# Router logits from the raw residual sum, with the norm folded into the router's weights, in a two-layer decoder on one core

## The reference

```python
x = layer_norm(DEEPNORM_ALPHA * x + mix, ln_g[i, 0], ln_b[i, 0])
ffn = grouped_moe(x, router_w, router_b, moe_w_gate[i], moe_w_up[i], moe_w_down[i])

def layer_norm(x, g, b):
    mu = jnp.mean(xf, axis=-1, keepdims=True)
    var = jnp.mean(jnp.square(xf - mu), axis=-1, keepdims=True)
    y = (xf - mu) * lax.rsqrt(var + LN_EPS)
    return y * g + b

# in grouped_moe
probs = jax.nn.softmax(h @ router_w + router_b, axis=-1)    # 32 experts
```

## Time and profile before

| | us |
|---|---|
| median of 3 runs | 1263.96 (1263.32 to 1266.03) |
| the profiled execution | 1266.65 |
| its span, first to last instruction | 1264.8 |
| TensorE busy | 1040.6 (82% of the span) |
| DVE busy | 289.6 (23%) |
| ACT busy | 173.6 (14%) |
| DMA moved | 450.95 MB, mean 357 GB/s |

### The profile page before, as it was taken

The page is one execution under the profiler, slowest core; times in us unless marked ns, Lnnn a source line. Parts: engine busy times, 40 slices in busy tenths (PEclk is TensorE's granted clock), DMA queues, the critical chain, the costliest instruction groups (busy, mean ns, idle before and its releaser), DMA issues.

```text
span 1264.8 us, 18155 instructions
## 1 busy us (share of the span) xinstructions
PE 1040.6 (82%) x7606; PEld 574.9 (45%) x7606; DVE 289.6 (23%) x848; ACT 173.6 (14%) x444; POOL 40.7 (3%) x106
## 2 busy tenths in 40 slices
PE   8999999876669886668899899999866698956675
PEld 6675544543334342233588654535523243523332
DVE  0026331211120211111322685312111111211113
ACT  0014210100000010000121452311100000000001
POOL 2001010000000000000000120100000000000000
PEclk9999999987889997898999899999978899988778
DMA  9943669999999999999985205699999999999994
GB/s 332 399 162 134 265 263 394 412 427 428 427 428 427 427 427 427 427 429 423 379 308 230 104 1 215 268 416 390 427 428 427 427 427 427 427 428 427 427 426 195
DMA packets 53298, 450.95 MB, mean 357 GB/s; under 512 B 4107, under 2 KB 10476, under 8 KB 26076
## 3 DMA queue, kind: packets, MB, share of 16 engines
q1 hardware_dynamic: 50864, 442.51, 84.8%
q0 software_dynamic: 2016, 6.81, 1.5%
q10 hardware_dynamic: 332, 0.40, 0.1%
HBM read 448.63 MB, written 1.07 MB: 356 GB/s over the span
## 4 chain that ended last, share of the span: by engine, by line
PE 47%; DMA 46%; DVE 3%; ACT 2%; issue 1%; SPq 1%; DVEq 0%
DMA ring<-in_moe_w_down 20%; DMA ring<-in_moe_w_up 15%; PE bank L825 12%; DMA ring<-in_moe_w_gate 11%; PE bank L628 7%; PE bank L703 5%; PE bank L876 3%; PE bank L794 3%; PE bank L865 3%; PE bank L635 2%; PE bank L1008 1%; PE bank L675 1%; PE bank L1075 1%; PE bank L1067 1%; PE bank L891 1%; PE bank L691 1%
## 5 line engine op out<-in xcount | busy, mean ns | idle before, releaser
L825 PE MATMUL bank<-ring,work 128*32 128x256 f32 (+1 forms) x2624 | 324.6, 468 | 75.3 <-DMA ring<-in_moe_w_up 35.0
L825 PEld LDWEIGHTS bank<-ring,work 128*32 128x32 f32 (+1 forms) x2624 | 150.9, 128 | 198.6 <-issue 168.5
L876 PE MATMUL bank<-ring,work 128*32 128x512 f32 x576 | 120.5, 784 | 39.0 <-DMA ring<-in_moe_w_down 23.4
L1360 DVE TENSOR_TENSOR xs<-xs,bank 128x512 f32<-128x512 f32 x120 | 76.5, 683 | 293.2 <-PE bank L894 216.0
L1352 DVE TENSOR_TENSOR work<-work,bank 128x256 f32<-128x256 f32 (+1 forms) x32 | 15.6, 488 | 392.3 <-PE bank L825 392.3
L825 PE MATMUL bank<-softmax_area,work 128*32 128x256 f32 (+1 forms) x416 | 67.6, 452 | 29.3 <-DMA ring<-in_moe_w_up 21.2
L628 PE MATMUL bank<-xT,ring 128*128 128x256 f32 x384 | 85.0, 381 | 0.0
L628 PEld LDWEIGHTS bank<-xT,ring 128*128 128x128 f32 x384 | 72.3, 190 | 11.0 <-issue 1.4
L794 PE MATMUL bank<-work,acc 128*128 128x128 f32 (+1 forms) x448 | 73.3, 321 | 4.3 <-DVE xs L1360 4.0
L794 PEld LDWEIGHTS bank<-work,acc 128*128 128x128 f32 x448 | 65.7, 191 | 16.6 <-issue 10.7
L876 PEld LDWEIGHTS bank<-ring,work 128*32 128x32 f32 x576 | 30.9, 137 | 85.7 <-issue 83.2
(11 more groups left out here) (217 smaller groups left out, 1023.1 us busy)
## 6 DMA issues: line engine op xcount, KB each, us to landing
ring<-in_moe_w_gate SPq DMA_DIRECT2D x48, 2048.0 KB, 28.5
ring<-in_moe_w_up SPq DMA_DIRECT2D x42, 2048.0 KB, 28.9
ring<-in_moe_w_down SPq DMA_DIRECT2D x36, 2048.0 KB, 29.8
ring<-in_moe_w_down SPq DMA_DIRECT2D x20, 1024.0 KB, 11.1
bias<-in_moe_w_down SPq DMA_DIRECT2D x8, 2048.0 KB, 32.4
softmax_area<-in_moe_w_down SPq DMA_DIRECT2D x8, 2048.0 KB, 21.1
bias<-in_moe_w_gate SPq DMA_DIRECT2D x8, 2048.0 KB, 31.7
softmax_area<-in_moe_w_up SPq DMA_DIRECT2D x8, 2048.0 KB, 28.4
```

The lines of the kernel that those rows point to most:

```text
L825: last = mm(bank[2 + k][row:row + cap, 0:width], xgT[:, t, at + e * cap:at + (e + 1) * cap], w[e](t)[:, part * width:(part + 1) * width], ...
L876: last = mm(bank[5][row:row + CAP_NARROW, :], hidT_narrow[:, m, CAP_NARROW * e:CAP_NARROW * (e + 1)], w[e](m)[:, n * 512:(n + 1) * 512], s ...
L1360: v.tensor_tensor(c, c, bank[b][:, :], ALU.add).then_inc(acc_added[l], 1)
```

## The change

The normed value of a token is (a - mean) r g + b, with a the raw sum and r the reciprocal deviation. Its product with the router's column is r times the product of a with a centred column, plus a constant. The centred column is g times the router's, less its own sum over features divided by 1024. The constant is the sum of b times the router's column. So the logits can be made from `acc`: the centred weights take the place of `router`, the constant goes into `logit_bias`, and r is multiplied in when DVE takes the logits from PSUM.

- `fold_router` on DVE: two multiplications and two reductions over the eight rows that a partition holds. `sum_router` on TensorE: one product with ones, which adds over partitions. `centre_router` on DVE: two operations. For layer 0 they stand before attention. For layer 1 they stand in pair 4 of layer 0's experts, and GpSimd loads `router_w` again before that.
- Two more small loads bring g and b of the two attention norms by feature (`norm_cols`).
- `norm_tile` leaves `acc` as it is and writes both passes to `xs`.
- TensorE transposes `acc` of tile 0 between the halves of tile 1's output products, and `acc` of tile 1 between the halves of tile 0's logits.
- On ACT the copy of tile 1 into `xT` stands before its square root, and the copy of tile 1 into `xsP` stands after the exponent.
- The wait for small loads is now for all nine.

```diff
...
@@ -547,6 +553,8 @@
             nc.gpsimd.memset(gate_w[:, KT * 3 * HEADS:], 0.0).then_inc(pads_ready, 1)
             pool.dma_start(router[:, 0:KT * E].rearrange("p (t n) -> p t n", t=KT),
                            router_w.rearrange("(p t) n -> p t n", t=KT)).then_inc(small_loaded, 16)
+            for w, src in enumerate((ln_g, ln_b)):
+                pool.dma_start(norm_cols[:, w, :, :], bass.AP(tensor=src.tensor, offset=0, ap=[[KT, P], [2 * D, LAYERS], [1, KT]])).then_inc(small_loaded, 16)
             pool.dma_start(router_bias[:, :], bass.AP(tensor=router_b.tensor, offset=0, ap=[[0, P], [1, E]])).then_inc(small_loaded, 16)
             for b, src in enumerate((nsa_pos_k, nsa_pos_v)):
                 pool.dma_start(pos_rows[:, b, :], src[0].rearrange("(l o) d -> l (o d)", o=2)).then_inc(small_loaded, 16)
@@ -591,6 +599,8 @@
                 load_norm(2 * l + 1)
                 order_columns(l)
                 if l + 1 < LAYERS:
+                    pool.wait_ge(logits_ready, l + 1)
+                    pool.dma_start(router_t, router_w.rearrange("(p t) n -> p t n", t=KT)).then_inc(small_loaded, 16)
                     load_norm(2 * l + 2)
 
 
@@ -602,12 +612,12 @@
                 u = ring_use["fixed", l, n, 0]
                 pe.wait_ge(loaded[slot_no(u)], loads_through(u))
 
-            def transpose_x(n, tt):
+            def transpose_x(n, tt, of=xs):
 
                 after(pe, xT_copied, 2 * (NT * n + tt))
                 for half in range(2):
                     for t in range(4):
-                        last = tr(bank[4 + half][:, t * P:(t + 1) * P], xs[:, tt, 4 * half + t::KT], ident)
+                        last = tr(bank[4 + half][:, t * P:(t + 1) * P], of[:, tt, 4 * half + t::KT], ident)
                     last.then_inc(xT_ready, 1)
 
             def xT_here(n, tt):
@@ -724,28 +734,40 @@
                     for n in range(2):
                         last = out_product(l, m, 1, n)
                 last.then_inc(mix_ready[l], 1)
+                pe.wait_ge(mix_added[l], 2)
+                transpose_x(2 * l + 1, 0, acc)
                 for n in range(2):
                     for m in range(KT // 2, KT):
                         last = out_product(l, m, 1, n)
                     last.then_inc(mix_ready[l], 1)
 
+            def sum_router(l, b):
+
+                pe.wait_ge(router_sums, l + 1)
+                mm(bank[b][:, 0:2 * E], table("ones"), router_red, start=True, stop=True).then_inc(router_psum, 1)
+
             def keep_warm(n, width=512):
 
                 for _ in range(n):
                     mm(bank[2][:, 0:width], ident, tab[:, 0:width], start=True, stop=True)
 
             def route_tokens(l):
-                for tt in range(NT):
-                    normed(l, 0, tt)
-                    transpose_x(2 * l + 1, tt)
-                    if tt == 0:
-                        pe.wait_ge(small_loaded, SMALL_LOADS)
-                        pe.wait_ge(pads_ready, 3)
-                    xT_here(2 * l + 1, tt)
-                    for t in range(KT):
+                def logits(tt, a, b):
+                    for t in range(a, b):
                         last = mm(bank[6][:, tt * P:(tt + 1) * P], xT[:, t, tt * P:(tt + 1) * P], router[:, t * E:t * E + P],
                                   start=(t == 0), stop=(t == KT - 1))
-                last.then_inc(logits_ready[l], 1)
+                    return last
+
+                pe.wait_ge(router_ready, l + 1)
+                pe.wait_ge(small_loaded, SMALL_LOADS)
+                pe.wait_ge(pads_ready, 3)
+                xT_here(2 * l + 1, 0)
+                logits(0, 0, KT // 2)
+                pe.wait_ge(mix_added[l], 4)
+                transpose_x(2 * l + 1, 1, acc)
+                logits(0, KT // 2, KT)
+                xT_here(2 * l + 1, 1)
+                logits(1, 0, KT).then_inc(logits_ready, 1)
                 keep_warm(5)
 
                 pe.wait_ge(chosen_ready[l], 1)
@@ -915,6 +937,9 @@
                     if more:
                         for part in range(2):
                             gather(l, group_of[i] + 1, part)
+                    if i == ROUTER_PAIR and l + 1 < LAYERS:
+                        sum_router(l + 1, 2)
+                        pe.wait_ge(router_ready, l + 2)
                 spread(l, PAIRS - 1)
                 if l + 1 < LAYERS:
                     keep_warm(4)
@@ -1021,6 +1046,8 @@
             first_groups()
             for g in range(2, 6):
                 moba_group(g)
+            sum_router(0, 7)
+
             def moba_job(h, br):
                 if h == 0:
                     pe.wait_ge(proj_dve[0], 3)
@@ -1247,13 +1274,33 @@
                 link(v.bn_aggr(moments[:, tt, :], stats[:, tt, :]))
                 v.tensor_scalar(rstd[:, tt:tt + 1], moments[:, tt, 1:2], EPS, None, ALU.add).then_inc(var_ready, 1)
 
+            def fold_router(l):
+
+                def cols_of(w):
+                    return norm_cols[:, w, l, :].unsqueeze(2).to_broadcast([P, KT, E])
+
+                def over_t(x):
+                    return x.rearrange("p t n -> p n t")
+
+                dve.wait_ge(small_loaded, SMALL_LOADS + 16 * l)
+                link(v.tensor_tensor(router_tmp, router_t, cols_of(1), ALU.mult))
+                link(v.tensor_reduce(router_red[:, E:2 * E], over_t(router_tmp), AX, ALU.add))
+                link(v.tensor_tensor(router_t, router_t, cols_of(0), ALU.mult))
+                v.tensor_reduce(router_red[:, 0:E], over_t(router_t), AX, ALU.add).then_inc(router_sums, 1)
+
+            def centre_router(l, b):
+                dve.wait_ge(router_psum, l + 1)
+                v.tensor_tensor(logit_bias[:, :], router_bias[:, :], bank[b][:, E:2 * E], ALU.add)
+                v.scalar_tensor_tensor(router_t, bank[b][:, 0:E].unsqueeze(1).to_broadcast([P, KT, E]), -1.0 / D, router_t,
+                                       ALU.mult, ALU.add).then_inc(router_ready, 1)
+
             def norm_tile(l, n, tt):
                 k = norm_tiles(l, n, tt)
                 dve.wait_ge(norm_loaded, 32 * (2 * l + n + 1))
-                v.scalar_tensor_tensor(acc[:, tt, :], acc[:, tt, :], moments[:, tt, 0:1], norm_w[:, 0, :], ALU.subtract, ALU.mult)
+                v.scalar_tensor_tensor(xs[:, tt, :], acc[:, tt, :], moments[:, tt, 0:1], norm_w[:, 0, :], ALU.subtract, ALU.mult)
                 dve.wait_ge(std_ready, k)
                 link(v.reciprocal(rstd[:, tt:tt + 1], rstd[:, tt:tt + 1]))
-                v.scalar_tensor_tensor(xs[:, tt, :], acc[:, tt, :], rstd[:, tt:tt + 1], norm_w[:, 1, :], ALU.mult, ALU.add).then_inc(normed_tiles, 1)
+                v.scalar_tensor_tensor(xs[:, tt, :], xs[:, tt, :], rstd[:, tt:tt + 1], norm_w[:, 1, :], ALU.mult, ALU.add).then_inc(normed_tiles, 1)
 
             def attention_norm(l):
                 for tt in range(NT):
@@ -1270,12 +1317,14 @@
                     return x.unsqueeze(2).to_broadcast([P, NT, E])
 
                 pr = route[:, 0, :, :]
-                dve.wait_ge(logits_ready[l], 1)
-                link(v.tensor_tensor(pr, bank[6][:, 0:NT * P].rearrange("p (t e) -> p t e", e=P)[:, :, 0:E],
-                                     router_bias[:, :].unsqueeze(1).to_broadcast([P, NT, E]), ALU.add))
+                dve.wait_ge(logits_ready, l + 1)
+                for tt in range(NT):
+                    last = v.scalar_tensor_tensor(pr[:, tt, :], bank[6][:, tt * P:tt * P + E], rstd[:, tt:tt + 1], logit_bias[:, :],
+                                                  ALU.mult, ALU.add)
+                link(last)
                 link(v.tensor_reduce(one[:, 0, :], pr, AX, ALU.max))
-                v.tensor_tensor(pr, pr, wide(one[:, 0, :]), ALU.subtract).then_inc(logits_shifted[l], 1)
-                dve.wait_ge(logits_exp[l], 1)
+                v.tensor_tensor(pr, pr, wide(one[:, 0, :]), ALU.subtract).then_inc(logits_shifted, 1)
+                dve.wait_ge(logits_exp, l + 1)
                 g4 = pr.rearrange("p t (g e) -> p t g e", e=EG)
                 for a in range(2):
                     v.tensor_tensor(pair_sum[:, :, :, a], g4[:, :, :, 2 * a], g4[:, :, :, 2 * a + 1], ALU.add)
@@ -1399,6 +1448,8 @@
                     more = last_of_group(i) and i + 1 < PAIRS
                     if i == FLAG_PAIR:
                         read_flag(l)
+                    if i == ROUTER_PAIR and l + 1 < LAYERS:
+                        fold_router(l + 1)
                     weigh(i)
                     if more:
                         choose_next(i)
@@ -1412,6 +1463,8 @@
                     if more:
                         for part in range(2):
                             copy_xg(group_of[i] + 1, part)
+                    if i == ROUTER_PAIR and l + 1 < LAYERS:
+                        centre_router(l + 1, 2)
             flag = {}
 
             def read_flag(l):
...
@@ -1614,9 +1669,11 @@
 
             def norm(l, n):
                 for tt in range(NT):
+                    if n == 0 and tt == 1:
```

(13 more changed lines are left out.)

13 lines of the change are left out of this document (9 added, 4 removed).

## The result

The changed kernel takes **1254.28 us** (median of 5, 1253.38 to 1257.72) where the kernel before took 1263.58 beside it (5 runs, 1262.9 to 1266.03): ratio 0.9923, 95% interval 0.991 to 0.9937, so by the ratio 9.7 us faster (8.0 to 11.4); the medians alone differ by 9.3. With e8, whose added delay its trace doesn't carry on, the mean is 9.2. The profiled execution of the changed kernel took 1253.38 us (span 1251.5) and was the fastest of its five; the profile of the kernel before came from an execution (1266.65) that was slower than each of its five. The 13.3 us between the two spans must not be read as the effect: 3 to 4 us of it are the difference between two executions.

A forecast was written before the change was run, and what follows sets the result against it. Experts' weights over DMA were taken to set the pace, started by pair 0's first freed slots. Paths gaining 9.5 us, less 0.7 for start loads and 0.3 for the reload, gave 8.5: 1263.96 to 1255.5 us, range 1253.5 to 1259.0.

The forecast's parts named there:

- What bounds the kernel: Expert weights' DMA sets the pace; pair 0's first freed slots shift the stream, so the path from output products to logits counts twice.
- Rival (c): At the expert stage: the DMA stream, not pair 0, opens it, so the shift does not carry; 1264 us, chance 5%.
- The new path: Last output product to logits: transposes and logits without waits, 5.05 us earlier in layer 0, DVE free 0.2 before the logits.
- (a): In tile 1's logits: TensorE still at 1.2 GHz, each layer loses 1.7 us; 1258.8 us, chance 10%.
- (e): On the routing path: DVE's passes are last all along, 1 to 2 us a layer; 1257.5 to 1259 us, chance 8%.
- The operation on the scaled logits: On DVE: scaling by the deviation makes one addition on 64 columns two operations, 0.17 us more.
- The sum of the two paths, 9.5: Routing paths of both layers: net 4.9 us gained in layer 0 and 4.6 in layer 1, together 9.5.
- The costs, 0.7 and 0.3: Two small loads at the start cost 0.7 us (0 to 2.0); the router's reload under full DMA costs 0.3 (0 to 0.6).
- The folds: DVE passes before layer 0's attention and in pair 4: zero cost; pair 4's last two under 1.4 us, TensorE at worst 1.5 late.
- The first slots: In the expert stage: the first slot freed about 4 us earlier in layer 0 and about 8.5 in layer 1.
- The range: Whole kernel: 1253.5 us (no start or reload cost 1254.5, and 0.7 of scatter) to 1259.0, which takes in the low-clock rival.
- The total: Whole kernel: 9.5 less 0.7 less 0.3 gives 8.5 us gained, so 1255.5 us; forecast case 63%.

The follow-up runs named there:

- e8: Changed kernel with ten more filling products (8.5 us of TensorE) at the end of pair 4 in layer 0; 1257.79 us, ratio 0.9937 to the kernel before.
- e7: Changed kernel with 15 filling products instead of 5 in layer 0's routing, ahead of the ranks; 1264.44 us, ratio 0.9991 to the kernel before.
- e4: The change in layer 0 alone; layer 1 has the old path and pair 4 no fold; 1258.84 us, ratio 0.9949 to the kernel before.
- e5: Changed kernel with the two norm_cols loads issued last, behind the gate weights; 1256.69 us, ratio 0.9927 to the kernel before.
- e11b: Changed kernel with six more norm-column loads at the start, into buffers that nothing reads; 1253.51 us, ratio 0.9914 to the kernel before.
- e1: Changed kernel with its added work kept but folded weights sent to scratch and the old routing path; 1263.51 us, ratio 0.9989 to the kernel before.
- e2: Changed kernel with raw-sum logits and ACT's new order, but neither set of transposes moved on TensorE; 1258.1 us, ratio 0.9938 to the kernel before.
- e6: Changed kernel with only the second move undone: tile 1's transposes behind all of tile 0's logits; 1256.98 us, ratio 0.9938 to the kernel before.
- e3: Kernel before with filling products in TensorE's waits for DVE and for ACT's copies; 1264.93 us, ratio 0.9998 to the kernel before.
- e9: Kernel before, unchanged, against itself; 1265.44 us, ratio 1.0003.
- e10: Changed kernel once more, unchanged, on the chip of its batch; 1254.49 us, ratio 0.993 to the kernel before.

## Why the prediction was right, step by step

- **What bounds the kernel.** Right. The routing path carries one to one (e7), the inside of the expert stage forgives a delay (e8), the two layers add up (e4). Rival (c), that the shift does not carry, is out.
- **The new path.** The events that were forecast on the path are there: no wait before tile 0's transposes, logits of tile 1 at the full clock, DVE free 0.29 before them (0.2 was said), the gather covering the move of ACT's copy. Last product to logits taken: 145.59 to 150.34, 4.75, plus 0.89 for the transposes, 5.64 against 10.82 before: 5.2 gained where 5.05 were forecast. Rivals (a) and (e) did not happen in any of the fifteen layers, though (e) was 0.28 us away.
- **The operation on the scaled logits** cost 0.19 more (0.42 for the earlier trace rows's 0.23), and 0.17 was said. The exponent no longer waits for a table load behind a copy: 0.33 back at the full clock, not foreseen. That is why the path from logits taken to slot became shorter at the full clock, 14.02 to 13.86, and not longer.
- **The sum of the two paths, 9.5.** Near in size, partly by luck. 3.1 of it (3.69 - 2.02 and 3.44 - 2.02 us) was tile 1's logits at the low clock, taken from one profile as a fixed property of the old order. It is an event of some executions: at the full clock the change is worth 23.17 - 19.46 = 3.71 in layer 1 and 23.51 - 19.46 = 4.05 in layer 0, 7.8 together, and 1.1 more on average for low stretches that did not come, 8.9. So the clock was booked 2.0 too high; the costs, also too high, and the unforeseen 0.36 for the ranks and 0.33 a layer for the exponent made up for it.
- **The costs, 0.7 and 0.3: the mis-sized terms.** The price of the two loads was taken from the shares of other small loads in GpSimd's queue, as if what they occupy were taken from the first weights. e5 and e11b put it at nothing: six more loads did not delay the first projection. The two shares of the earlier trace rows can't carry a price either. The same windows of the changed kernel, 8 to 10 us and then 5 to 11.5:

```profile
q0 software_dynamic: 67, 0.02, 57.0%
...
q0 software_dynamic: 251, 0.21, 28.5%
```

From 8 to 10 us the share is 57.0% for 12.8%, but over 5 to 11.5 us 28.5% for 27.8%: the queue is not busier, its busiest stretch has moved. From 6 to 8 us it falls from 65.7% to 28.0%, and e11b with its eight loads has only 12.1% from 8 to 10. The first projection began at 10.94 (11.55 in the earlier trace rows), earlier than the 11.5 to 13.5 that were forecast. The reload shows nowhere: X0 is 440.9 to 441.6 with and without it, in all profiles but e5's (443.7, for which the runs show no reason). The estimate from the Trainium skill (DMA: Bandwidth & Descriptors, sections Specifications and Bandwidth), 1.4 us for the two loads and so 1256.2, lies above the measured median, and by e5 and e11b the two loads cost this kernel nothing. What such a transfer takes by itself no run here shows.
- **The folds.** Layer 0's passes took 0.41, 0.59, 0.42 and 0.59 from 48.00 on, the last two 0.19 and 0.42 from 54.42, and DVE waited 1.13 for scores behind them. In pair 4 of layer 0 the last passes end at 284.49 and TensorE took gate weights after a wait for DMA. The timeline of the changed kernel, which answers to the earlier trace rows:

```profile
281.58 2.48 DVE L1409 TENSOR_TENSOR xs<-xs,bank 128x512 f32<-128x512 f32 x4 [12.11 <-PE bank L916]
283.98 0.18 DVE L1293 TENSOR_TENSOR logit_bias<-router_bias,bank 128x32 f32<-128x32 f32 x1
284.07 0.42 DVE L1294 SCALAR_TENSOR_TENSOR router<-bank,router 128x256 f32<-128x256 f32 x1
...
285.03 0.60 PE L847 MATMUL bank<-softmax_area,work 128*32 128x256 f32 x1 [2.33 <-DMA ring<-in_moe_w_gate]
```

The passes take 0.6, under the bound of 1.4, and the weights came later still. Zero in both layers, as e1 says too.
- **The first slots.** They were to come about 4 and 8.5 us earlier and came 6.9 and 13.3 earlier. Of the 13.3 the two paths are 10.0; the other 3.3 lie in A, X0 and A1, where the change has nothing but the 0.89 a layer already counted, so they are the difference between two executions.
- **The range.** Its lower end doesn't follow from its own terms: 1254.5 less 0.7 is 1253.8, not 1253.5. The measured 1254.28 is inside either way, 0.2 from the 1254.5 that the prediction gives for costs of nothing.
- **The total.** 8.5 was forecast, 9.5 to 9.7 measured. Without the 1.0 of costs the forecast would have been 9.5. What the runs support is 8.9 from the traces and 0.6 to 0.8 that they don't place, less than the interval of any ratio. The timed gains of e1, e2 and e4 also lie 1.0, 2.5 and 1.8 us above what their traces add up to; e6, on another chip, lies 0.4 above. e1, e2 and e4 were timed on one chip, and its runs of the kernel before may have read high by some 1.5. But e3 was timed there too and lies 0.9 below what its trace adds up to, which speaks against this. The cause stays open.

## What to carry to other kernels

Find the place from which the bound resource is set going and price only what stands ahead of it; 8.5 us of the same work moved the first slot by 7.65 there (8.6 by the timed ratios), and 130 us later by the trace nothing. When a norm stands between a sum and a small matmul, fold its scale and mean into the matmul's weights: here that took the wait for the norm off the path, 1.9 us a layer, and with the transposes moved into TensorE's other work 1.8 more. Do not price a transfer from a queue's share in a window of 2 us, since the share moves between windows from kernel to kernel. And before a slow stretch in one profile is booked as a gain, look at a second profile of the same kernel: the low clock that I counted as 3.1 us was there in three layers of seven.

## What the runs showed of the hardware

- **The granted clock differs between executions of the same program**, at the same waits. With waits of 1.5 and 0.7 us before them, tile 1's logits ran mostly at 1.2 GHz in both layers of one profile of the kernel before (3.69 us at a granted clock of 0.54, and 3.44) and at 2.4 GHz in both layers of e9 (1.00, 2.05 us), whose layer 0 then had a lower clock in the next stage (0.69). At the head of layer 1's attention the window 700 to 720 us has 1.00 in seven profiles and 0.83 in seven, whatever the kernel; A1 is 173.3 to 175.9 us in the first and 175.4 to 178.1 in the second. The same 20 us, in the changed kernel and in e8 (windows):

```profile
700.00:720.00 20.00, 15.85 (x122) 10.04 (x121) 17.42 (x87) 11.36 (x46) 3.72 (x5) 1.00 0.28 106
```

```profile
700.00:720.00 20.00, 17.33 (x105) 12.07 (x103) 11.91 (x59) 9.31 (x38) 2.66 (x4) 0.83 0.29 106
```

- **Spans of single profiles are no measure of a change of 1%.** Kernels with the whole change and timed ratios within 0.0016 had profiled spans from 1249.3 to 1257.6 (e10, e5).
- **Without a wait TensorE did not lose the clock on this path.** In the fifteen layers with both moves R is 18.56 to 18.58 us, the delayed one of e7 left out. That the missing waits are the reason is not shown: the four layers of e2 and e6, where TensorE still waits 0.7 to 0.8 us for ACT's copies, didn't lose it either (R 21.23 to 21.24 and 19.28 to 19.29). The window from tile 0's first logits to tile 1's last, in the changed kernel:

```profile
145.43:150.34 4.91, 4.91 (x42) 4.80 (x41) 4.29 (x8) 2.46 (x4) 0.00 (x0) 1.00 0.77 270
```
